# The sum of squares of four RMSNorms moved into the steps that produce the residual, in a hybrid decoder layer

## The chip, the cores and the metric

The kernel runs on all 8 cores of one Trainium2 chip. Two cores share one sequence of 8192 tokens; each has 4096 tokens, and 128 tokens ahead of them (the halo), whose keys, values and conv state it needs. There is no exchange between cores. The metric is the device time of the slowest core, in microseconds (us).

## The reference

One layer over `x` of (4, 8192, 1024), float32, then a final RMSNorm:

```
h = x + 1/2 * SwiGLU_1(RMSNorm(x))                      # d_ff 2816
u = RMSNorm(h);  q,k,v,B,C,xc = u @ W_in
attn = sliding_window_attention(rope(q), rope(k), v)    # window 128, blocks of 128
conv = B * causal_depthwise_conv3(C * xc)
h = h + concat(RMSNorm(attn), RMSNorm(conv)) @ W_out
h = h + CrossAttn(RMSNorm(h), RMSNorm(mem))             # 256 memory tokens
h = h + 1/2 * SwiGLU_2(RMSNorm(h))
out = RMSNorm(h)
# RMSNorm(x) = x * rsqrt(mean(x*x) + 1e-5) * gain, over the 1024 features
```

## The kernel before

**Layout.** A core works in 4 passes of 1024 tokens. The residual `h` stays in SBUF as float32 with features on partitions: 8 chunks of 128 features by 1024 tokens. A pass is cut into two sub-tiles of 512 tokens (`SUB`), s = 0 and 1. Weights stream through a ring in SBUF, by POOL's DMA queue; a load waits until TensorE is done with what stood there. `x` and the output go by SP's queue in blocks of 128 tokens, each through two staging buffers. In pass 0 the halo's 128 tokens are a third, small sub-tile (`hh`, `uh`, `acth`) in FFN1 and in the mixer's input.

**A pass.** `ffn` (norm, input product, SiLU gate, output product), `mixer` (norm, input product with rotary and conv, attention, output product), `xattn` (norm, query product, attention, output product), `ffn` again, `final_out`. The input product of an FFN is 11 weight tiles with 64 matmuls each (4 groups of 8 for the gate and 8 for the product), the longest dense stretch of a pass.

**A norm.** `rmsnorm_to_u` runs for every sub-tile ahead of the stage that uses it. It calls `rms_stats_fm`: for each of the 8 feature chunks, ScalarE squares the chunk into one of two bf16 buffers (`tmpb`), and TensorE multiplies it by a matrix of ones, which adds over the partitions and leaves the sum in all of them, accumulated over the chunks in one PSUM bank. Then Ln and Exp on ScalarE give the reciprocal root (`lnv`, `rstd`), and 8 `scalar_tensor_tensor` on VectorE write `u = h * gain * rstd`. Squares of one sub-tile and scalings of the other may run side by side. The helpers record the operation, so in the profile every matmul is L366, every activation L384, a transpose L370, a copy L406 (ScalarE) or L407 (VectorE).

**The residual loops.** The output products of FFN1, mixer, cross-attention and FFN2 run over m (8 output chunks) and then over s: a group of 22 (FFN) or 8 matmuls of 512 columns into one PSUM bank, and VectorE adds it to `h` (`h` L401 in the FFNs, `h` L388 in the other two). Banks 0 to 5 rotate; 6 and 7 belong to the attention's output.

**The block loops.** `load_x` (pass 0) and `final_out` (between passes) take 8 blocks of 128 tokens. `x_tr` transposes a block of `x` in two halves of four 128x128 pieces, and copies half 0 by VectorE and half 1 by ScalarE into `h`. `final_out` first transposes `h` back for the output (`identf,h`), squares it on ScalarE with a row sum, adds the two sums (`small`), takes Ln and Exp, multiplies by the gain (`stage<-ps,small,gfin`) and sends the block out; then it calls `x_tr` for the next pass's block.

**What sets the order.** Each engine runs its instructions in the order in which the program records them, and waits by semaphores for what the recorder found an operation to need. There is no scheduler: where a matmul stands in the code is where it stands in TensorE's queue.

```
def rms_stats_fm(src_chunks, n, nfeat):
    ...
    for i, s in enumerate(src_chunks):
        sq = nxt("tmpb", tmpb)[:, 0:n]
        act_fn(sq, s, AF.Square)
        mm(ssp, ones, sq, i == 0, i == nchunk - 1)
```

Of the kernel before, what the change touches and what calls it, by code (L numbers as in the profile page):

```python
# [9 lines left out]
AF = mybir.ActivationFunctionType  # L10
# [210 lines left out]
def build_program(cfg):  # L221
# [63 lines left out]
    a = [scr_addr]  # L285
# [221 lines left out]
    def x_dma(row0):  # L507
        stg = nxt("xstage", xstage)
        ldma(stg[:, :], x_d.ap()[row0:row0 + 128, :])
        return stg  # L510

    def x_tr(stg, hdst, bi):
        for half in range(2):
            b = bank()
            for q in range(4):
                kc = half * 4 + q
                tr(ps[:, b, q * 128:(q + 1) * 128], stg[:, kc * 128:(kc + 1) * 128], identf[:, :])
            v_copy(hdst[:, half * 4:half * 4 + 4, bi * 128:(bi + 1) * 128],
                   ps[:, b, :].rearrange("p (a c) -> p a c", a=4), eng=("act" if half else "dve"))

    def load_x(row0, nblocks, hdst):
        for bi in range(nblocks):
            x_tr(x_dma(row0 + bi * 128), hdst, bi)

    def ffn(subs, gcol, wi_d, wo_d, hook=None):
        for (hs, us, as_, n) in subs:
            rmsnorm_to_u(hs, us, n, gcol)
        hooks = list(hook()) if hook is not None else []
        for ti in range(FC // 2):
            wt = wtile(KC * 512)  # L530
            wv = wt[:, :].rearrange("p (k n) -> p k n", k=KC)
            wdma(wv[:, :, 0:256], wsrc(wi_d, 0, KC, ti * 256, 256))
            wdma(wv[:, :, 256:512], wsrc(wi_d, 0, KC, DFF + ti * 256, 256))
            for cc in range(2):
                c = ti * 2 + cc
                for (hs, us, as_, n) in subs:
                    bg, bu = bank(), bank()
                    for kc in range(KC):
                        mm(ps[:, bg, 0:n], wv[:, kc, cc * 128:(cc + 1) * 128], us[:, kc, :], kc == 0, kc == KC - 1)
                    for kc in range(KC):  # L540
                        mm(ps[:, bu, 0:n], wv[:, kc, 256 + cc * 128:256 + (cc + 1) * 128], us[:, kc, :], kc == 0, kc == KC - 1)
                    sg = nxt("sgb", sgb)[:, 0:n]
                    act_fn(sg, ps[:, bg, 0:n], AF.Silu)
                    v_tt(as_[:, c, :], sg, ps[:, bu, 0:n], ALU.mult)
            if ti >= 1 and hooks:
                hooks.pop(0)()
        while hooks:
            hooks.pop(0)()
        for tj in range(4):
            wt = wtile(FC * 256)  # L550
            wv = wt[:, :].rearrange("p (k n) -> p k n", k=FC)
            wdma(wv[:, 0:11, :], wsrc(wo_d, 0, 11, tj * 256, 256))
            wdma(wv[:, 11:22, :], wsrc(wo_d, 11 * 128, 11, tj * 256, 256))
            for mmi in range(2):
                m = tj * 2 + mmi
                for (hs, us, as_, n) in subs:
                    b = bank()
                    for kc in range(FC):
                        mm(ps[:, b, 0:n], wv[:, kc, mmi * 128:(mmi + 1) * 128], as_[:, kc, :], kc == 0, kc == FC - 1)
                    v_stt(hs[:, m, :], ps[:, b, 0:n], 0.5, hs[:, m, :], ALU.mult, ALU.add)  # L560

    def rope_tables(col0, ncols, pos_col0):
        thunks = []
# [51 lines left out]
    def mixer(p_idx, main_subs, halo):  # L615
        if halo:
            rmsnorm_to_u(hh, uh, HALO, GC_MIX)
        for (c0, n) in main_subs:
            rmsnorm_to_u(h[:, :, c0:c0 + n], u[:, :, c0:c0 + n], n, GC_MIX)
        toks = []  # L620
        if halo:
            toks.append((uh, HALO, 0, True, None))
# [176 lines left out]
        for tj in range(4):  # L799
            wt = wtile(KC * 256)  # L800
            wv = wt[:, :].rearrange("p (k n) -> p k n", k=KC)
            for g in range(2):
                src = wmo_d.ap()[g * 256:(g + 1) * 256, tj * 256:(tj + 1) * 256].rearrange("(j d) n -> d j n", d=64)
                wdma(wv[g * 64:(g + 1) * 64, 0:4, :], src)
            wdma(wv[:, 4:8, :], wsrc(wmo_d, 512, 4, tj * 256, 256))
            for mmi in range(2):
                m = tj * 2 + mmi
                for (c0, n) in main_subs:
                    b = bank()
                    for kc in range(KC):  # L810
                        mm(ps[:, b, 0:n], wv[:, kc, mmi * 128:(mmi + 1) * 128], bufA[:, kc, c0:c0 + n], kc == 0, kc == KC - 1)
                    v_tt(h[:, m, c0:c0 + n], ps[:, b, 0:n], h[:, m, c0:c0 + n], ALU.add)

    def xattn(main_subs):
        for (c0, n) in main_subs:
            rmsnorm_to_u(h[:, :, c0:c0 + n], u[:, :, c0:c0 + n], n, GC_XATT)
        for tj in range(4):
            wt = wtile(KC * 256)
            wv = wt[:, :].rearrange("p (k n) -> p k n", k=KC)
# [97 lines left out]
    out_ops = []

    def final_out(p_idx, next_load):
        nrow0 = HALO + (p_idx + 1) * T  # L920
        pre = [x_dma(nrow0 + i * 128) for i in range(min(2, NBLK))] if next_load else []
        for bi in range(NBLK):
            stg = nxt("stage", stage)
            bks = [bank(), bank()]
            sm = nxt("small", small)
            for half in range(2):
                for q in range(4):
                    kc = half * 4 + q
                    tr(ps[:, bks[half], q * 128:(q + 1) * 128], h[:, kc, bi * 128:(bi + 1) * 128], identf[:, :])
                act_fn(stg[:, half * 512:(half + 1) * 512], ps[:, bks[half], :], AF.Square, accum=sm[:, half:half + 1])  # L930
            v_tt(sm[:, 2:3], sm[:, 0:1], sm[:, 1:2], ALU.add)
            act_fn(sm[:, 3:4], sm[:, 2:3], AF.Ln, scale=1.0 / D, bias=epsc[:, :])
            act_fn(sm[:, 2:3], sm[:, 3:4], AF.Exp, scale=-0.5)
            for half in range(2):
                v_stt(stg[:, half * 512:(half + 1) * 512], ps[:, bks[half], :], sm[:, 2:3],
                      gfin[:, half * 512:(half + 1) * 512], ALU.mult, ALU.mult)
            r0 = p_idx * T + bi * 128
            o = P.dma("sp", out_d.ap()[r0:r0 + 128, :], stg[:, :], reads=[stg[:, :]])
            out_ops.append(o)
            if next_load:  # L940
# [159 lines left out]
```

How the kernel before makes its waits and increments, by code:

```python
    def emit(self, eng, h, final_wait=()):  # L194
        seen = {}
        for o in self.ops[eng]:
            need = {}
            for d in o.deps:
                assert d.val is not None
                k = d.sem
                if seen.get(k.num, 0) >= d.val:
                    continue
                if need.get(k.num, (None, 0))[1] < d.val:
                    need[k.num] = (k, d.val)
            for num, (k, v) in need.items():
                h.wait_ge(k, v)
                seen[num] = v
            if o.is_dma:
                out, in_ = o.fn
                h.dma_start(out=out, in_=in_).then_inc(o.sem, 16)
            else:
                ins = o.fn(h)
                if o.signals:
                    ins.then_inc(o.sem, 1)
        for d in final_wait:
            if seen.get(d.sem.num, 0) < d.val:
                h.wait_ge(d.sem, d.val)
                seen[d.sem.num] = d.val
```

## Time and profile before

| | us |
|---|---|
| median of 6 runs | 3741.78 |
| lowest, highest run | 3737.97, 3843.55 |
| the profiled execution's own time | 3741.16 |
| its span on the slowest core (core 1) | 3739.6 |
| TensorE busy, VectorE, ScalarE, POOL | 3234.0, 1411.8, 1008.8, 341.0 |
| spans of the 8 cores | 3732.4 to 3739.6 |
| mean granted TensorE clock of core 1 | 0.869 |

The spans of all cores lie within 0.2%. A granted clock of 1.00 is 2.4 GHz and 0.50 is 1.2 GHz; the engine was always at one of the two. "Busy" TensorE in a row includes the end of each matmul, which overlaps the next one's start, so a busy share says less than the spacing of the starts.

### The profile page before, as it was taken

Reading aid. Unit: us, or ns where it says so; the run is one execution under the profiler, and the core shown is the slowest. Engines: PE = TensorE matmul, PEld = TensorE weight load, DVE = VectorE, ACT = ScalarE, POOL = GpSimd, SP = SyncE. Lnnn points to the kernel's source line nnn. Section 1 sums busy time; section 2 is a strip of 40 time slices with the busy share of each in tenths; the row PEclk is TensorE's granted clock in tenths of the full one; section 3 lists DMA queues with packets and bytes.
Section 4 is the critical chain, followed back from the end, with each engine's and each line's share of the span. In section 5 each row is a group of like instructions: output and inputs, shape, how many; then the busy total and the mean of one; then the engine's idle time right before and its main releaser. Section 6 shows DMA issues by size and latency. Waiting matters only on the chain.

```text
span 3739.6 us, 47167 instructions; the slowest of 8 cores (3732.4 to 3739.6 us)
## 1 busy us (share of the span) xinstructions
PE 3234.0 (86%) x15098; PEld 1449.3 (39%) x15098; DVE 1411.8 (38%) x3210; ACT 1008.8 (27%) x2442; POOL 341.0 (9%) x391
## 2 busy tenths in 40 slices
PE   4999868899899877889979977879997997688997
PEld 2454323344444332334444433323443443233444
DVE  1431654421243355441134145453114415544212
ACT  2220253421131125341031024442103102534211
POOL 1011100011101110001101110000110111000110
PEclk7999957799999985879989997679998998577998
DMA  9456312256746540426656643124664665022453
GB/s 159 53 76 74 37 15 25 33 60 74 127 69 86 66 51 1 46 23 79 73 116 94 77 48 35 18 29 50 79 74 111 79 75 54 11 27 31 62 72 76
DMA packets 405726, 228.52 MB, mean 61 GB/s; under 512 B 56944, under 2 KB 396528, under 8 KB 405488
## 3 DMA queue, kind: packets, MB, share of 16 engines
q0 software_dynamic: 393392, 186.67, 43.3%
q1 hardware_dynamic: 12096, 38.83, 3.1%
q8 instruction: 130, 2.13, 0.2%
q14 instruction: 108, 0.88, 0.1%
HBM read 395.35 MB, written 16.78 MB: 110 GB/s over the span
## 4 chain that ended last, share of the span: by engine, by line
PE 73%; ACT 9%; DVE 9%; issue 6%; DMA 2%; DVEq 0%; ACTq 0%; SPq 0%; POOLq 0%
PE ps L366 72%; ACT tmpb L384 3%; DVE u L401 2%; ACT pf L384 2%; ACT pT L406 1%; PE ps L370 1%; DVE bufA L401 1%; DVE small L845 1%; DMA out<-stage 1%; ACT lnv L384 1%; DVE small L717 1%; DMA xstage<-x 1%; DVE pb L394 1%; ACT rstd L384 1%; DVE small L414 1%
## 5 line engine op out<-in xcount | busy, mean ns | idle before, releaser
L366 PE MATMUL ps<-u,wt 128*128 128x512 bf16 x7744 | 1732.6, 385 | 16.3 <-DVE u L401 16.1
L366 PEld LDWEIGHTS ps<-u,wt 128*128 128x128 bf16 x7744 | 764.5, 99 | 956.7 <-issue 88.1
L366 PE MATMUL ps<-act,wt 128*128 128x512 bf16 x2816 | 610.2, 379 | 0.0
L388 DVE TENSOR_TENSOR act<-sgb,ps 128x512 bf16<-128x512 f32 x352 | 240.4, 687 | 809.8 <-PE ps L366 786.5
L384 ACT ACTIVATE sgb<-ps 128x512 f32<-128x512 f32 (+1 forms) x374 | 213.6, 578 | 804.9 <-PE ps L366 792.2
L366 PEld LDWEIGHTS ps<-act,wt 128*128 128x128 bf16 x2816 | 275.2, 98 | 330.4
L366 PE MATMUL ps<-tmpb,cbf 128*128 128x512 bf16 (+1 forms) x473 | 175.0, 428 | 179.8 <-ACT tmpb L384 138.9
L210 POOL DMA_DIRECT2D wt<-w_ffn_in x176 | 154.3, 879 | 1562.0 <-PE ps L366 1557.9
L401 DVE SCALAR_TENSOR_TENSOR h<-ps,h 128x512 f32<-128x512 f32 x128 | 88.6, 692 | 522.1 <-PE ps L366 522.1
L384 ACT ACTIVATE tmpb<-h 128x512 bf16<-128x512 f32 x256 | 148.6, 623 | 467.2 <-PE ps L366 369.8
L401 DVE SCALAR_TENSOR_TENSOR u<-h,gains,rstd 128x512 bf16<-128x512 f32 x256 | 172.5, 746 | 128.9 <-ACT rstd L384 128.9
L384 ACT ACTIVATE pf<-ps,small 128x257 f32<-128x257 f32 (+1 forms) x384 | 184.4, 481 | 47.3 <-DVE small L414 28.4
L366 PE MATMUL ps<-cbf,pb 128*128 128x128 bf16 x768 | 141.4, 288 | 55.6 <-DVE pb L394 47.2
L366 PEld LDWEIGHTS ps<-tmpb,cbf 128*128 128x128 bf16 x473 | 45.7, 107 | 331.9 <-issue 327.3
L406 ACT CAST pT<-ps 128x256 bf16<-128x256 f32 x384 | 142.2, 373 | 103.3 <-PE ps L366 92.8
L394 DVE TENSOR_SCALAR pb<-pf,small 128x256 bf16<-128x256 f32 x384 | 135.5, 353 | 30.4 <-DVE small L414 2.8
L388 DVE TENSOR_TENSOR h<-ps,h 128x512 f32<-128x512 f32 x128 | 88.6, 692 | 141.9 <-PE ps L366 141.9
L384 ACT ACTIVATE stage<-ps 128x512 f32<-128x512 f32 x64 | 38.3, 599 | 339.1 <-PE ps L370 312.4
L717 DVE TENSOR_REDUCE small<-ps 128x1 f32<-128x257 f32 x256 | 106.9, 420 | 49.8 <-PE ps L366 49.4
L210 POOL DMA_DIRECT2D wt<-w_ffn_out x64 | 67.9, 1061 | 579.7 <-PE ps L366 579.7
L366 PE MATMUL ps<-bufA,wt 128*128 128x512 bf16 x512 | 118.0, 395 | 0.0
L366 PEld LDWEIGHTS ps<-cbf,pb 128*128 128x128 bf16 x768 | 63.6, 119 | 120.9 <-issue 107.2
(126 smaller groups left out, 2091.2 us busy)
## 6 DMA issues: line engine op xcount, KB each, us to landing
wt<-w_ffn_in POOLq DMA_DIRECT2D x176, 512.0 KB, 8.6
wt<-w_ffn_out POOLq DMA_DIRECT2D x64, 704.0 KB, 9.3
xstage<-x SPq DMA_DIRECT2D x33, 512.0 KB, 6.0
out<-stage SPq DMA_DIRECT2D x32, 512.0 KB, 2.9
wt<-w_mix_in POOLq DMA_DIRECT2D x48, 256.0 KB, 7.5
wt<-w_xq POOLq DMA_DIRECT2D x16, 512.0 KB, 7.3
wt<-w_xo POOLq DMA_DIRECT2D x16, 512.0 KB, 7.5
wt<-w_mix_in POOLq DMA_DIRECT2D x12, 512.0 KB, 8.6
```

The source lines that it names most:

```text
L210: h.dma_start(out=out, in_=in_).then_inc(o.sem, 16)
L366: return P.op("pe", lambda e: e.matmul(out, lhsT=lhsT, rhs=rhs, start=start, stop=stop), reads=[lhsT, rhs], writes=[out])
L370: return P.op("pe", lambda e: e.transpose(out, in_, ident), reads=[in_, ident], writes=[out])
L384: return P.op("act", lambda e: e.activation(out=out, in_=in_, func=func, scale=scale, **kw), reads=reads, writes=writes)
L388: return P.op("dve", lambda e: e.tensor_tensor(out=out, in0=in0, in1=in1, op=op), reads=[in0, in1], writes=[out])
L394: return P.op("dve", lambda e: e.tensor_scalar(out=out, in0=in0, scalar1=s1, scalar2=None, op0=op0), reads=reads, writes=[out])
L401: return P.op("dve", lambda e: e.scalar_tensor_tensor(out=out, in0=in0, scalar=scalar, in1=in1, op0=op0, op1=op1), reads=reads, writes=[out])
L406: return P.op("act", lambda e: e.copy(out=out, in_=in_), reads=[in_], writes=[out])
L414: return P.op("dve", lambda e: e.reciprocal(out=out, in_=in_), reads=[in_], writes=[out])
L717: P.op("dve", lambda e: e.tensor_reduce(out=sm[:, 0:1], in_=ps[:, b, 0:257], axis=AX.X, op=ALU.max, negate=True), reads=[ps[:, b, 0:257]], ...
L845: P.op("dve", lambda e: e.tensor_reduce(out=sm[:, 0:1], in_=ps[:, b, 0:MEM], axis=AX.X, op=ALU.max, negate=True), reads=[ps[:, b, 0:MEM]], ...
```

## The change

`stats_add` squares one chunk and issues its ones-matmul; `stats_finish` is Ln and Exp on the finished sum. The sums now stand in PSUM bank 6 + s. The residual loops of FFN1, mixer and cross-attention call `stats_add` after each add; `x_tr` squares and sums each half of a block as it is loaded. `rmsnorm_to_u` then only finishes. The halo sub-tile and the final norm keep the old way. The number of squared elements is the same; for the loaded `x` the ones-matmuls are 64 of 128 columns per pass where they were 16 of 512.

```diff
+    def stats_add(s, m, chunk_ap, n):
+        sq = nxt("tmpb", tmpb)[:, 0:n]
+        act_fn(sq, chunk_ap, AF.Square)
+        mm(ps[:, 6 + s, 0:n], ones, sq, m == 0, m == KC - 1)
+
+    def stats_finish(s, n, nfeat):
...
+        act_fn(lv, ps[:, 6 + s, 0:n], AF.Ln, scale=1.0 / nfeat, bias=epsc[:, :])
+        act_fn(rs, lv, AF.Exp, scale=-0.5)
+        return rs
...
-    def rmsnorm_to_u(hsrc, udst, n, gcol):
-        rs = rms_stats_fm([hsrc[:, kc, :] for kc in range(KC)], n, D)
+    def rmsnorm_to_u(hsrc, udst, n, gcol, fused_s=None):
+        if fused_s is None:
+            rs = rms_stats_fm([hsrc[:, kc, :] for kc in range(KC)], n, D)
+        else:
+            rs = stats_finish(fused_s, n, D)
...
-            v_copy(hdst[:, half * 4:half * 4 + 4, bi * 128:(bi + 1) * 128],
-                   ps[:, b, :].rearrange("p (a c) -> p a c", a=4), eng=("act" if half else "dve"))
+            dst = hdst[:, half * 4:half * 4 + 4, bi * 128:(bi + 1) * 128]
+            v_copy(dst, ps[:, b, :].rearrange("p (a c) -> p a c", a=4), eng=("act" if half else "dve"))
+            if fuse:
+                s = (bi * 128) // SUB
+                cc0 = (bi * 128) % SUB
+                sq = nxt("tmpb", tmpb)[:, 0:512].rearrange("p (a c) -> p a c", a=4)
+                act_fn(sq, dst, AF.Square)
+                for q in range(4):
+                    kc = half * 4 + q
+                    mm(ps[:, 6 + s, cc0:cc0 + 128], ones, sq[:, q, :], kc == 0, kc == KC - 1)
...
                     v_stt(hs[:, m, :], ps[:, b, 0:n], 0.5, hs[:, m, :], ALU.mult, ALU.add)
+                    if fuse_next and fs is not None:
+                        stats_add(fs, m, hs[:, m, :], n)
...
                     v_tt(h[:, m, c0:c0 + n], ps[:, b, 0:n], h[:, m, c0:c0 + n], ALU.add)
+                    stats_add(c0 // SUB, m, h[:, m, c0:c0 + n], n)
...
-                x_tr(pre[bi], h, bi)
+                x_tr(pre[bi], h, bi, fuse=True)
```

TensorE's order at the end of FFN1 in pass 1, before (`act,wt` are the output product's matmuls, `tmpb,cbf` the ones-matmuls):

```order
L366 MATMUL ps<-act,wt_182 128x512 x88
L366 MATMUL ps<-act,wt_183 128x512 x88
L366 MATMUL ps<-act,wt_184 128x512 x88
L366 MATMUL ps<-act,wt_185 128x512 x88
L366 MATMUL ps<-tmpb_83,cbf 128x512
L366 MATMUL ps<-tmpb_82,cbf 128x512
```

and with the change:

```order
L366 MATMUL ps<-act,wt_182 128x512 x22
L366 MATMUL ps<-tmpb_83,cbf 128x512
L366 MATMUL ps<-act,wt_182 128x512 x22
L366 MATMUL ps<-tmpb_82,cbf 128x512
L366 MATMUL ps<-act,wt_182 128x512 x22
L366 MATMUL ps<-tmpb_83,cbf 128x512
```

A ones-matmul now stands behind every 22 matmuls, where 16 stood together behind all 352. The mixer's and the cross-attention's loops read alike with groups of 8.

TensorE's order in `final_out` between two passes, before:

```order
L370 MATMUL ps<-identf,h 128x128 x8
L370 MATMUL ps<-identf,xstage_67 128x128 x8
L370 MATMUL ps<-identf,h 128x128 x8
L370 MATMUL ps<-identf,xstage_66 128x128 x8
L370 MATMUL ps<-identf,h 128x128 x8
```

and with the change:

```order
L370 MATMUL ps<-identf,h 128x128 x8
L370 MATMUL ps<-identf,xstage_67 128x128 x4
L366 MATMUL ps<-tmpb_83,cbf 128x128 x4
L370 MATMUL ps<-identf,xstage_67 128x128 x4
L366 MATMUL ps<-tmpb_82,cbf 128x128 x4
L370 MATMUL ps<-identf,h 128x128 x8
```

Between the two halves of an `x` block, and between it and the next block of `h`, four ones-matmuls stand now.

## Rows read from the trace of the kernel before

**Rows 1.** The page, busy us of each engine, share of the span, instructions.
```profile
PE 3234.0 (86%) x15098; PEld 1449.3 (39%) x15098; DVE 1411.8 (38%) x3210; ACT 1008.8 (27%) x2442; POOL 341.0 (9%) x391
```

**Rows 2.** Timeline, mixer out to queries: start, us, engine, line, operation, count [idle <-releaser].
```profile
1528.93 0.59 PE L366 MATMUL ps<-tmpb,cbf 128*128 128x512 bf16 x2
...
1529.20 0.69 DVE L388 TENSOR_TENSOR h<-ps,h 128x512 f32<-128x512 f32 x1 [1.03 <-PE ps L366]
...
1533.67 0.69 ACT L384 ACTIVATE lnv<-ps,epsc 128x512 f32<-128x512 f32 x1 [0.62 <-PE ps L366]
...
1535.18 5.39 DVE L401 SCALAR_TENSOR_TENSOR u<-h,gains,rstd 128x512 bf16<-128x512 f32 x8 [5.29 <-ACT rstd L384]
...
1542.84 5.39 DVE L401 SCALAR_TENSOR_TENSOR u<-h,gains,rstd 128x512 bf16<-128x512 f32 x8 [2.26 <-ACT rstd L384]
...
1548.37 24.55 PE L366 MATMUL ps<-u,wt 128*128 128x512 bf16 x113 [0.28 <-DVE u L401]
```

**Rows 3.** Timeline, pass 1, FFN1's output product to the mixer's input.
```profile
1276.73 0.59 PE L366 MATMUL ps<-tmpb,cbf 128*128 128x512 bf16 x2
...
1281.48 1.28 ACT L384 ACT_TABLE_LOAD   x1 [0.62 <-PE ps L366]
...
1297.48 0.38 PE L366 MATMUL ps<-u,wt 128*128 128x512 bf16 x1 [0.29 <-DVE u L401]
...
1299.05 3.20 PE L366 MATMUL ps<-u,wt 128*128 128x512 bf16 x8
```

**Rows 4.** Timeline, pass 1, the hand-offs between engines around the mixer's output product.
```profile
1498.43 0.60 ACT L384 ACTIVATE tmpb<-ps 128x512 bf16<-128x512 f32 x1 [1.27 <-PE ps L366]
...
1499.18 0.59 PE L366 MATMUL ps<-tmpb,cbf 128*128 128x128 bf16 x4 [0.84 <-ACT tmpb L384]
...
1503.28 0.69 DVE L388 TENSOR_TENSOR h<-ps,h 128x512 f32<-128x512 f32 x1 [1.42 <-PE ps L366]
...
1504.07 0.63 ACT L384 ACTIVATE tmpb<-h 128x512 bf16<-128x512 f32 x1 [3.44 <-DVE h L388]
```

**Rows 5.** Timeline, pass 1, TensorE at a matmul of the rotary embedding.
```profile
1303.13 0.38 PE L366 MATMUL ps<-tmpb,cbf 128*128 128x512 bf16 x1 [0.88 <-ACT tmpb L406]
```

**Rows 6.** Timeline, block loop between passes 1 and 2, to FFN1's input product.
```profile
1897.98 1.04 PE L370 MATMUL ps<-identf,h 128*128 128x128 f32 x8
...
1912.65 1.91 PE L370 MATMUL ps<-identf,h 128*128 128x128 f32 x8
...
1915.51 0.16 DVE L388 TENSOR_TENSOR small<-small 128x1 f32<-128x1 f32 x1 [2.02 <-ACT stage L384]
...
1916.46 1.41 DVE L401 SCALAR_TENSOR_TENSOR stage<-ps,small,gfin 128x512 f32<-128x512 f32 x2 [0.79 <-ACT small L384]
...
1917.79 0.68 DVE L407 COPY h<-ps 128x512 f32<-128x512 f32 x1
...
1954.01 8.36 PE L366 MATMUL ps<-u,wt 128*128 128x512 bf16 x38 [0.29 <-DVE u L401]
```

**Rows 7.** Timeline, pass 0: first load of `x` to FFN1's input product.
```profile
60.20 3.69 PE L370 MATMUL ps<-identf,xstage 128*128 128x128 f32 x16 [8.20 <-DMA xstage<-x]
...
61.39 0.69 DVE L407 COPY h<-ps 128x512 f32<-128x512 f32 x1 [9.03 <-PE ps L370]
...
83.56 0.59 ACT L406 COPY h<-ps 128x512 f32<-128x512 f32 x1 [2.38 <-PE ps L370]
...
88.46 2.19 DVE L401 SCALAR_TENSOR_TENSOR uh<-hh,gains,rstd 128x128 bf16<-128x128 f32 x8 [5.05 <-ACT rstd L384]
...
109.28 2.10 PE L366 MATMUL ps<-u,wt 128*128 128x512 bf16 x9 [0.29 <-DVE u L401]
```

**Rows 8.** Windows (rotary, attention): us; PE, PEld, DVE, ACT, POOL busy; clock; DMA.
```profile
1303.13:1318.40 15.27, 10.88 (x46) 4.37 (x46) 10.26 (x16) 2.94 (x5) 2.64 (x3) 1.00 0.57 52
1388.00:1498.00 110.00, 77.77 (x371) 30.39 (x371) 59.02 (x222) 62.81 (x213) 0.00 (x0) 0.50 0.00 1
```

More of the change, by code:

```diff
@@ L461, in rms_stats_fm @@
         return rs
-    def rmsnorm_to_u(hsrc, udst, n, gcol):
-        rs = rms_stats_fm([hsrc[:, kc, :] for kc in range(KC)], n, D)
+    assert NSUB <= 2
+    def stats_add(s, m, chunk_ap, n):
[3 more added lines that the diff above has]
+    def stats_finish(s, n, nfeat):
+        i_ = rr.get("rstd", 0)
+        rr["rstd"] = i_ + 1
+        lv = lnv[i_ % 2][:, 0:n]
+        rs = rstd[i_ % 2][:, 0:n]
+        act_fn(lv, ps[:, 6 + s, 0:n], AF.Ln, scale=1.0 / nfeat, bias=epsc[:, :])
[6 more added lines that the diff above has]
+            rs = stats_finish(fused_s, n, D)
         for kc in range(KC):
@@ L510, in x_dma, with x_tr @@
         return stg
-    def x_tr(stg, hdst, bi):
+    def x_tr(stg, hdst, bi, fuse=False):
         for half in range(2):
@@ L517, in x_tr, with load_x, ffn @@
                 tr(ps[:, b, q * 128:(q + 1) * 128], stg[:, kc * 128:(kc + 1) * 128], identf[:, :])
-            v_copy(hdst[:, half * 4:half * 4 + 4, bi * 128:(bi + 1) * 128],
-                   ps[:, b, :].rearrange("p (a c) -> p a c", a=4), eng=("act" if half else "dve"))
-    def load_x(row0, nblocks, hdst):
+            dst = hdst[:, half * 4:half * 4 + 4, bi * 128:(bi + 1) * 128]
[8 more added lines that the diff above has]
+                    mm(ps[:, 6 + s, cc0:cc0 + 128], ones, sq[:, q, :], kc == 0, kc == KC - 1)
+    def load_x(row0, nblocks, hdst, fuse=False):
         for bi in range(nblocks):
[L523 to L527, printed above, removed]
+            x_tr(x_dma(row0 + bi * 128), hdst, bi, fuse=fuse)
+    def ffn(subs, gcol, wi_d, wo_d, hook=None, fuse_next=False):
+        for (hs, us, as_, n, fs) in subs:
+            rmsnorm_to_u(hs, us, n, gcol, fused_s=fs)
         hooks = list(hook()) if hook is not None else []
@@ L535, in ffn @@
                 c = ti * 2 + cc
-                for (hs, us, as_, n) in subs:
+                for (hs, us, as_, n, fs) in subs:
                     bg, bu = bank(), bank()
@@ L555, in ffn @@
                 m = tj * 2 + mmi
-                for (hs, us, as_, n) in subs:
+                for (hs, us, as_, n, fs) in subs:
                     b = bank()
@@ L618, in mixer @@
         for (c0, n) in main_subs:
-            rmsnorm_to_u(h[:, :, c0:c0 + n], u[:, :, c0:c0 + n], n, GC_MIX)
+            rmsnorm_to_u(h[:, :, c0:c0 + n], u[:, :, c0:c0 + n], n, GC_MIX, fused_s=c0 // SUB)
         toks = []
@@ L812, in mixer @@
                     v_tt(h[:, m, c0:c0 + n], ps[:, b, 0:n], h[:, m, c0:c0 + n], ALU.add)
+                    stats_add(c0 // SUB, m, h[:, m, c0:c0 + n], n)
     def xattn(main_subs):
         for (c0, n) in main_subs:
-            rmsnorm_to_u(h[:, :, c0:c0 + n], u[:, :, c0:c0 + n], n, GC_XATT)
+            rmsnorm_to_u(h[:, :, c0:c0 + n], u[:, :, c0:c0 + n], n, GC_XATT, fused_s=c0 // SUB)
         for tj in range(4):
@@ L915, in xattn @@
                     v_tt(h[:, m, c0:c0 + n], ps[:, b, 0:n], h[:, m, c0:c0 + n], ALU.add)
+                    stats_add(c0 // SUB, m, h[:, m, c0:c0 + n], n)
     out_ops = []
@@ L950, in build_program @@
             load_x(0, 1, hh)
-            load_x(HALO, NBLK, h)
+            load_x(HALO, NBLK, h, fuse=True)
             hook = lambda: rope_tables(0, TP, 0)
@@ L959, in build_program @@
         if halo:
-            subs.append((hh, uh, acth, HALO))
+            subs.append((hh, uh, acth, HALO, None))
         for (c0, n) in main_subs:
-            subs.append((h[:, :, c0:c0 + n], u[:, :, c0:c0 + n], act[:, :, c0:c0 + n], n))
-        ffn(subs, GC_FFN1, w1i_d, w1o_d, hook=hook)
+            subs.append((h[:, :, c0:c0 + n], u[:, :, c0:c0 + n], act[:, :, c0:c0 + n], n, c0 // SUB))
+        ffn(subs, GC_FFN1, w1i_d, w1o_d, hook=hook, fuse_next=True)
         mixer(p_idx, main_subs, halo)
         xattn(main_subs)
-        subs2 = [(h[:, :, c0:c0 + n], u[:, :, c0:c0 + n], act[:, :, c0:c0 + n], n) for (c0, n) in main_subs]
+        subs2 = [(h[:, :, c0:c0 + n], u[:, :, c0:c0 + n], act[:, :, c0:c0 + n], n, c0 // SUB) for (c0, n) in main_subs]
         ffn(subs2, GC_FFN2, w2i_d, w2o_d)
```

## The prediction

> **What bounds the kernel now.** I read the page first: TensorE is busy 86% of a span of 3739.6 us, the other engines below 40% [rows 1]. So what counts is what holds TensorE up. Next I read the timeline around one norm, the mixer's exit into the cross-attention (pass 1), since the change touches norms. TensorE's last output matmul ends at about 1528.93 us, where the norm's own ones-matmuls begin; the scaling of `u` for sub-tile 0 starts at 1535.18, for sub-tile 1 at 1542.84, and the last matmul that waits for such a `u` starts at 1548.37: the norm holds the dense stream up for 19.44 us [rows 2]. The same norm after FFN1 takes 20.75 us, with a table load of 1.28 us ahead of its Ln [rows 3]. The one ahead of FFN2 looks like the first. Last I read what a dependent matmul costs an in-order TensorE [rows 4, 5], and the two loops that load `x` [rows 6, 7].
>
> A difference of under 0.2% (7.5 us) can't be told from no change here. The sum is made against the profiled execution's own 3741.16 us, which lies 0.6 us under the median of the six runs shown.
>
> **Residual loops (FFN1 out, mixer out, cross-attention out).** For each output chunk m and sub-tile s, the stream was 22 or 8 matmuls, then the next group's. Now one ones-matmul stands between them, and it needs this group's own result: last matmul, the add on VectorE, Square on ScalarE, ones-matmul. TensorE has nothing else in its queue, since the next group's matmuls stand behind. The wait, from rows:
> - last matmul's start to the start of the add: 0.49 us. The ones-matmul at 1528.93 started as the last output matmul had streamed its 0.217 us (113 matmuls in 24.55 us), and the add started at 1529.20 [rows 2];
> - the add 0.69 us; 0.10 to the Square; Square 0.63 [rows 4];
> - Square's end to the ones-matmul: 0.15 (1498.43 + 0.60 to 1499.18) [rows 4];
> - the ones-matmul itself: 0.22.
>
> That is 2.28 us from the last matmul of a group to the first of the next, where it was 0.22: **2.06 us more per group**, 1.84 of it idle. There are 16 groups per loop, 3 loops, 4 passes. The last group's wait I count with the norm behind it, so 15 x 3 x 4 = 180 groups: **+371 us**. That presumes TensorE at 2.4 GHz. The add and the Square cost nothing more: ScalarE was idle in these loops and VectorE did the add before. No DMA is moved, and POOL's weight loads, which wait for TensorE to free the ring, merely come later with it. PSUM banks 6 and 7, which hold the sums now, are used by attention alone and free by then.
>
> **The norms behind these loops.** The 16 Squares and ones-matmuls go; Ln, Exp and the 16 scalings stay. From the end of the last output matmul (t = 0), cross-attention case: add 0.27 to 0.96, Square 1.06 to 1.69, ones-matmul at 1.84. Ln of sub-tile 0 needs none of this and stands behind the last Square in ScalarE's queue, so it starts at 1.69. From Ln's start to the scaling is 1.51 us (1533.67 to 1535.18), so `u` of sub-tile 0 starts at 3.20, and Ln and Exp of sub-tile 1 hide beside it. Now VectorE is the bound: 8 scalings in 5.39 us, then 8 more, the last awaited matmul 5.53 us after their start (1542.84 to 1548.37) [rows 2]: 3.20 + 5.39 + 5.53 = 14.1 us instead of 19.44. After FFN1 the table load comes first: 15.4 instead of 20.75 [rows 3]. So a norm gives back only 5.3 us, not the 10 us of Squares taken out, because the Squares of sub-tile 1 already ran beside the scaling of sub-tile 0. 12 norms: **-64 us**.
>
> **The block loop between passes** (`final_out` with the next load, 8 blocks, 3 times). Before, the transposes of `x` run ahead of ScalarE and VectorE; with the norm behind it, the stretch from the first transpose to the last awaited matmul is 1897.98 to 1954.01, 56.0 us [rows 6]. Now each half's ones-matmuls wait for that half's copy and Square. With the clock at 1.2 GHz, which TensorE's little work here makes likely, one block from its first transpose: 2.86 us to the add of the two halves' sums (1912.65 to 1915.51), 0.95 to the gain multiply (to 1916.46), 1.33 to the copy of half 0 (to 1917.79) [rows 6]; copy 0.68, hand-off 0.10, Square 0.63, hand-off 0.15, four ones-matmuls about 0.43; four transposes to the copy about 1.2 (as 60.20 to 61.39 [rows 7]), copy 0.59, 0.10, Square 0.63, 0.15, 0.43. Sum 10.2 us; at 2.4 GHz the same comes to 8.8. Eight blocks to the last Square (the first still at the higher clock, with one table load) are 80.6 us, and the norm behind it now 1.6 + 5.39 + 5.53 = 12.5: 93 against 56, **+37 us** each, +111 in all; at the higher clock +28 each. The output DMAs have more time, not less.
>
> **The first load.** Its second block is in at 60.2 us, its last copy starts at 83.56 [rows 7]. A fused block takes about 3.2 + 3.1 = 6.3 us by the pieces above, so the seven from there end at 104 instead of 84. From there the halo norm's 4.4 us (to 88.46) and its scaling 2.2 stay, then 5.4 + 5.5: 121 against 109.28, **+12 us** (0 if the early loads hide it, 20 if they add to it).
>
> **The clock.** A fused norm feeds TensorE one matmul per 0.66 us for 11 us. Before, such a stretch of some 4 us ended at 1.2 GHz after FFN1: the next 8 matmuls took 3.20 us instead of 1.73 [rows 3]. Where the clock had come back before the dense stream (the other 12 norms, those ahead of FFN1 included), I charge one such stretch, 1.7 us: **+20 us** (0 to 40).
>
> Sum: 371 - 64 + 111 + 12 + 20 = +450, so **4190 us**. The case's own ends: down to 4117 with the boundary at 2.4 GHz (-27), no clock charge (-20), the load free (-12) and 1.98 us per group (-14); up to 4250 with both clock charges double (+20, and +16 for a slow second group at the start of the mixer's and the cross-attention's loops), 2.12 us per group (+11) and the load at 20 (+8).
>
> **Rivals.**
> 1. *The clock falls in the short loops.* In mixer out and cross-attention out TensorE would stream 1.95 of 3.79 us. For it: the attention loop with TensorE "busy" 77.77 of 110 us had a granted clock of 0.50 [rows 8]. Against: the rotary stretch, idle 0.88 us in each 3 us, had 1.00 [rows 5, 8]; my loop lies between. At 1.2 GHz a group takes 7 x 0.43 + 0.70 + 0.69 + 0.10 + 0.63 + 0.15 + 0.43 = 5.7 us, 1.9 more; 120 groups: +230, 4420 us. The Trainium skill ("TensorE: Matmul & The Clock Gate", A second HAM failure mode) has a rule that speaks for this rival: small idles between groups of matmuls, taken often enough, make the gate swing between its two levels. By it the short loops would lose all or part of those 230 us; the trace agrees for attention and not for the rotary stretch. Chance 6%.
> 2. *The block loops hide the waits.* If they were set by ScalarE's work alone, two more Squares of 0.63 per block would cost 10 us and the shorter norm give back 8: 4075 us. Against it, each piece of the chain waits for the one before. Chance 3%.
> 3. *The waits are covered, and the kernel gets faster.* If TensorE ran the next group's matmuls while the ones-matmul waits, the residual loops would keep their time, the norms give back 64, the block loops and the first load 32, less 20 for the clock: about 3665 us. It decides in the residual loops together with the block loop: with only the former covered the rest still adds 79; with both, the break-even lies at 0.4 us per group. Against: in the rotary stretch the next group's matmuls stand ready behind a matmul that waits for ScalarE, and TensorE idles 0.88 us all the same [rows 5]. Chance 3%, of which 1 within 0.2%.
>
> **Numbers.** The forecast has 88%. The range 4120 to 4260 holds its own ends nearly; left out are the three rivals (12%) and its own tail. Faster 2%, within 0.2% 1%, slower 97%.
>
> **What would show it.** In the waits, TensorE for ScalarE's `tmpb` should stand at over 400 us in total; the residual loops should show groups 3.8 us (8 matmuls) and 6.8 us (22) apart with granted clock 1.00; rows like those of 1542.84 should start 5.4 us after the first scaling; a block between passes 9 to 10 us. Groups 1.8 us apart, or 5.7, would make me wrong, and so would a block under 6 us.

## The result, and the profile after

| | before | with the change |
|---|---|---|
| median of the runs, us | 3739.74 (6 runs, 3737.97 to 3743.49) | 4193.56 (5 runs, 4189.34 to 4194.18) |
| ratio, with its 95% interval | | 1.121 [1.1195, 1.1226] |
| span of the core that is read, us | 3739.6 | 4186.4 |

The change makes the kernel 12% slower. The forecast was 4190 us. Some runs of every kernel show a lower granted clock and longer spans on one die or both; times and means over cores leave those runs and dies out, and the rows of after are of core 0 because cores 4 to 7 were like that in its execution. An experiment below that has no ratio rests on one or two runs.

The page's head and busy line, and the group of the ones-matmuls (last two numbers: idle time ahead of them in all, and what of it ScalarE's `tmpb` ended):

```profile
span 4186.4 us, 47522 instructions; the slowest of 8 cores (4185.2 to 4382.4 us)
...
PE 3301.0 (79%) x15290; PEld 1476.3 (35%) x15290; DVE 1411.0 (34%) x3210; ACT 1019.8 (24%) x2442; POOL 340.3 (8%) x391
...
L366 PE MATMUL ps<-tmpb,cbf 128*128 128x128 bf16 (+1 forms) x665 | 161.9, 333 | 594.9 <-ACT tmpb L384 559.2
```

Against [rows 1] no engine has much more to do: VectorE is where it was, ScalarE has 11 us more, and TensorE has 192 matmuls more (the 128-column ones of the block loops) and 67 us more busy time. The span grew by 447 us, so 380 of them are idle time of TensorE. The waits say for what (engine, what it waits for, us in total, times, longest):

```profile
PE ps L366 <- ACT tmpb L384: 559.2, 311, 6.0
ACT tmpb L384 <- DVE h L388: 417.2, 128, 5.1
ACT tmpb L384 <- DVE h L401: 413.5, 64, 7.9
```

The first row was 138.9 us in 170 waits before (its longest 3.5 us). The three rows are one ring: TensorE waits for the Square, the Square for the add, and the add, in rows not shown, for TensorE.

**Residual loops.** TensorE in FFN1's output product (start, us, operation, count, idle and its releaser):

```profile
1366.65 0.38 PE L366 MATMUL ps<-tmpb,cbf 128*128 128x512 bf16 x1 [1.78 <-ACT tmpb L384]
1366.86 4.91 PE L366 MATMUL ps<-act,wt 128*128 128x512 bf16 x22
1373.55 0.38 PE L366 MATMUL ps<-tmpb,cbf 128*128 128x512 bf16 x1 [1.78 <-ACT tmpb L384]
1373.76 4.91 PE L366 MATMUL ps<-act,wt 128*128 128x512 bf16 x22
1380.45 0.38 PE L366 MATMUL ps<-tmpb,cbf 128*128 128x512 bf16 x1 [1.78 <-ACT tmpb L384]
```

Every 22 matmuls are followed by 1.78 us in which TensorE is idle; groups stand 6.90 us apart. The hand-offs of one group of the mixer's output product, in time order over three engines:

```profile
1675.25 0.69 DVE L388 TENSOR_TENSOR h<-ps,h 128x512 f32<-128x512 f32 x1 [3.19 <-PE ps L366]
1676.15 0.63 ACT L384 ACTIVATE tmpb<-h 128x512 bf16<-128x512 f32 x1 [3.25 <-DVE h L388]
...
1676.92 0.38 PE L366 MATMUL ps<-tmpb,cbf 128*128 128x512 bf16 x1 [1.77 <-ACT tmpb L384]
...
1677.13 1.89 PE L366 MATMUL ps<-bufA,wt 128*128 128x512 bf16 x8
```

The add ends at 1675.94 and the Square starts at 1676.15, 0.21 us later, where [rows 4] have 0.10. Windows of FFN1 out, mixer out, cross-attention out, and six blocks of the block loop (us; busy and count of PE, PEld, DVE, ACT, POOL; granted clock; DMA share; GB/s):

```profile
1332.30:1440.93 108.63, 81.57 (x367) 35.30 (x366) 11.07 (x16) 9.44 (x15) 10.50 (x11) 1.00 0.48 55
1672.00:1720.00 48.00, 25.64 (x110) 10.47 (x111) 8.37 (x13) 8.18 (x13) 2.62 (x3) 1.00 0.28 33
1821.00:1875.00 54.00, 29.23 (x126) 11.65 (x125) 9.69 (x14) 8.81 (x14) 3.49 (x4) 1.00 0.34 39
1103.09:1163.57 60.48, 27.48 (x146) 23.02 (x145) 13.00 (x24) 22.31 (x54) 0.00 (x0) 0.50 0.29 102
```

The granted clock is 1.00, that is 2.4 GHz, in these windows of all three residual loops, with TensorE busy for 25.64 of 48.00 us in the second; in the block loop it is 0.50, that is 1.2 GHz. The windows of the mixer and the cross-attention leave out the first group of the loop, which still runs slowly behind the attention:

```profile
1660.50 3.23 PE L366 MATMUL ps<-bufA,wt 128*128 128x512 bf16 x8
```

Eight matmuls take 3.23 us there instead of 1.89. The kernel before has the same slow start (granted clock 0.94 over its whole loop), so it costs the change nothing.

**The norm behind the mixer**, which answers to [rows 2]:

```profile
1719.92 1.89 PE L366 MATMUL ps<-bufA,wt 128*128 128x512 bf16 x8
...
1721.92 0.69 DVE L388 TENSOR_TENSOR h<-ps,h 128x512 f32<-128x512 f32 x1 [3.19 <-PE ps L366]
...
1722.82 0.63 ACT L384 ACTIVATE tmpb<-h 128x512 bf16<-128x512 f32 x1 [3.25 <-DVE h L388]
...
1723.35 0.67 ACT L384 ACTIVATE lnv<-ps,epsc 128x512 f32<-128x512 f32 x1
...
1723.59 0.38 PE L366 MATMUL ps<-tmpb,cbf 128*128 128x512 bf16 x1 [1.78 <-ACT tmpb L384]
...
1724.85 10.69 DVE L401 SCALAR_TENSOR_TENSOR u<-h,gains,rstd 128x512 bf16<-128x512 f32 x16 [2.23 <-ACT rstd L384]
```

The last output matmul has streamed by 1721.66 (1719.92 and eight times 0.217). All 16 scalings run without a gap from 1724.85 to 1735.54, so from the end of that matmul to the last `u` it is 13.9 us, with the hand-off to TensorE about 14.0, where it was 19.44. VectorE is now the bound of the norm. What it does to the clock, in windows from the first matmul on the new `u`:

```profile
1725.74:1735.60 9.86, 8.77 (x15) 1.54 (x15) 9.86 (x16) 0.30 (x1) 0.00 (x0) 0.50 0.17 20
1735.60:1741.00 5.40, 5.32 (x20) 2.22 (x20) 1.23 (x2) 0.71 (x2) 0.47 (x1) 0.75 0.00 0
1741.00:1760.00 19.00, 19.00 (x90) 8.59 (x88) 4.15 (x6) 2.94 (x6) 3.03 (x4) 1.00 0.70 77
```

While each matmul waits for a scaling the clock stands at 0.50, which costs nothing: a scaling comes every 0.67 us and a matmul takes 0.43. In the 5.40 us behind, 20 matmuls run where 5.40 / 0.217 = 25 would: 1.1 us lost.

**The block loop**, which answers to [rows 6]: one block, and the last norm behind the loop.

```profile
1163.57 1.91 PE L370 MATMUL ps<-identf,h 128*128 128x128 f32 x8
...
1166.43 0.16 DVE L388 TENSOR_TENSOR small<-small 128x1 f32<-128x1 f32 x1 [7.08 <-ACT stage L384]
...
1167.37 1.41 DVE L401 SCALAR_TENSOR_TENSOR stage<-ps,small,gfin 128x512 f32<-128x512 f32 x2 [0.79 <-ACT small L384]
...
1168.70 0.68 DVE L407 COPY h<-ps 128x512 f32<-128x512 f32 x1
...
1169.47 0.63 ACT L384 ACTIVATE tmpb<-h 128x512 bf16<-128x512 f32 x1 [2.20 <-DVE h L407]
...
1170.25 0.58 PE L366 MATMUL ps<-tmpb,cbf 128*128 128x128 bf16 x4 [3.91 <-ACT tmpb L384]
...
1174.48 10.69 DVE L401 SCALAR_TENSOR_TENSOR u<-h,gains,rstd 128x512 bf16<-128x512 f32 x16 [4.80 <-ACT rstd L384]
...
1185.32 4.91 PE L366 MATMUL ps<-u,wt 128*128 128x512 bf16 x22 [0.29 <-DVE u L401]
```

The transposes of `h` start at 1103.09 and, six blocks on, at 1163.57: 10.1 us a block. From the first transpose of the loop (1092.23) to the last matmul that waits for a scaling (1185.32) it is 93.1 us, where it was 56.0 [rows 6]. Every step stands behind the one before it, 5.13 us to the copy of half 0 (1163.57 to 1168.70) and 1.55 from there to its ones-matmuls.

### The profile page after: what moved, and what is told of

The parts are those of the page before. It is cut to its first block, busy times and chain, and to the rows that moved or that the text cites. A ratio compares the mean times of both kernels' runs of the same rounds, so it can differ in the third digit from the quotient of the medians.

```text
span 4382.4 us, 47522 instructions; the slowest of 8 cores (4185.2 to 4382.4 us)
## 1 busy us (share of the span) xinstructions
PE 3500.0 (80%) x15290; PEld 1523.8 (35%) x15290; DVE 1411.0 (32%) x3210; ACT 1019.7 (23%) x2442; POOL 341.8 (8%) x391
## 3 DMA queue, kind: packets, MB, share of 16 engines
q8 instruction: 131, 2.15, 0.2%
## 4 chain that ended last, share of the span: by engine, by line
PE 71%; DVE 11%; ACT 10%; issue 7%; DMA 1%; ACTq 0%; DVEq 0%; SPq 0%; POOLq 0%
PE ps L366 69%; ACT tmpb L384 4%; DVE h L388 2%; PE ps L370 2%; ACT pf L384 2%; DVE h L401 1%; ACT pT L406 1%; DVE small L875 1%; DVE bufA L401 1%; DVE u L401 1%; DVE small L746 1%; DVE pb L394 1%; DVE small L414 1%; ACT lnv L384 1%; ACT stage L384 1%
## 5 line engine op out<-in xcount | busy, mean ns | idle before, releaser
L366 PE MATMUL ps<-u,wt 128*128 128x512 bf16 x7744 | 1899.6, 406 | 46.8 <-DVE u L401 35.4
L366 PEld LDWEIGHTS ps<-u,wt 128*128 128x128 bf16 x7744 | 789.3, 102 | 1107.1 <-issue 507.4
L366 PE MATMUL ps<-act,wt 128*128 128x512 bf16 x2816 | 666.6, 400 | 0.0
L366 PE MATMUL ps<-tmpb,cbf 128*128 128x128 bf16 (+1 forms) x665 | 167.7, 342 | 594.1 <-ACT tmpb L384 558.4
L366 PEld LDWEIGHTS ps<-act,wt 128*128 128x128 bf16 x2816 | 285.8, 102 | 357.8 <-issue 125.3
L384 ACT ACTIVATE tmpb<-h 128x512 bf16<-128x512 f32 x256 | 161.1, 629 | 988.9 <-DVE h L388 468.4
L366 PEld LDWEIGHTS ps<-tmpb,cbf 128*128 128x128 bf16 x665 | 60.4, 114 | 778.8 <-issue 777.6
L366 PE MATMUL ps<-bufA,wt 128*128 128x512 bf16 x512 | 164.8, 480 | 0.0
```

The lines of the kernel that those rows point to most:

```text
L366: return P.op("pe", lambda e: e.matmul(out, lhsT=lhsT, rhs=rhs, start=start, stop=stop), reads=[lhsT, rhs], writes=[out])
L384: return P.op("act", lambda e: e.activation(out=out, in_=in_, func=func, scale=scale, **kw), reads=reads, writes=writes)
```

## The experiments

Nine kernels, each against the kernel before. A ratio has its 95% interval.

**1. The residual loops alone.** The block loops and the first load keep the old way, and FFN1's norm squares for itself. **2. The loads alone**, the complement: `stats_add` out of the three residual loops.

```diff
 # 1
-            rmsnorm_to_u(hs, us, n, gcol, fused_s=fs)
+            rmsnorm_to_u(hs, us, n, gcol, fused_s=(None if fuse_next else fs))
-                x_tr(pre[bi], h, bi, fuse=True)
+                x_tr(pre[bi], h, bi)
-            load_x(HALO, NBLK, h, fuse=True)
+            load_x(HALO, NBLK, h)
 # 2
-                    stats_add(c0 // SUB, m, h[:, m, c0:c0 + n], n)
-                        stats_add(fs, m, hs[:, m, :], n)
```

> Only the residual loops of FFN1, mixer and cross-attention are fused; the loaded x is squared ahead of FFN1 as before. Theory (TensorE waits behind each ones-matmul): 180 groups at 2.06 to 2.13 us, 371 to 385, less 64 for the 12 norms, plus up to 20 for the clock: about 4070 us, 4045 to 4090. If the block loops carried more of the loss than I worked out, this run would come out under 4000.

> Only the block loops (first load and between passes) are fused; residual loops and the other norms as before. Theory: 37 us for each of 3 block loops and 12 for the first load, 3 to 5 for the clock: about 3870 us, 3850 to 3880. Its difference and that of the residual-only run should add up to the whole change's 451 us within 10. If the block loop hides the waits: 3750.

Measured: 4072.78 us and 3859.14 us, one run each, against 3738.79 before on the same chip. The excesses are 334 and 120 us; together 454, and the change as a whole has 454 (4193.56 less 3739.74). The two parts add up, and each lies where its theory had it. In the waits TensorE's wait for `tmpb` is 418.1 us with the residual loops alone and 278.4 us with the loads alone.

**3. The ones-matmul one group later.** Kernel 1, but a group's ones-matmul is issued behind the matmuls of the next group, ahead of that group's add. All Squares, ones-matmuls and sums are the same; only the place in TensorE's queue differs.

```diff
-        mm(ps[:, 6 + s, 0:n], ones, sq, m == 0, m == KC - 1)
+        late.append((ps[:, 6 + s, 0:n], sq, m == 0, m == KC - 1))
+
+    def stats_late():
+        while late:
+            o_, sq_, a_, b_ = late.pop(0)
+            mm(o_, ones, sq_, a_, b_)
...
+                    stats_late()
                     v_tt(h[:, m, c0:c0 + n], ps[:, b, 0:n], h[:, m, c0:c0 + n], ALU.add)
                     stats_add(c0 // SUB, m, h[:, m, c0:c0 + n], n)
```

> As the residual-only run, but each ones-matmul is issued one group later, behind the next group's 22 or 8 matmuls. Theory (the loss is the wait and nothing else): the waits are covered except the last of a loop, so the norms' gain remains: 3742 - 64 + up to 20 = 3680 to 3700 us. Rival (the loss is the interruption itself: the ones-matrix loaded into the array among the weights, the extra PSUM bank or the clock): it stays near the residual-only run, over 4000 us.

Measured: 3725.07 us (3722.40 to 3727.34), ratio 0.9964 [0.995, 0.9977]. The wait is gone, and with it 348 us; but the time misses its range by 25 us on the slow side. TensorE in the mixer's output product:

```profile
1522.92 0.38 PE L366 MATMUL ps<-tmpb,cbf 128*128 128x512 bf16 x1
1523.15 1.89 PE L366 MATMUL ps<-bufA,wt 128*128 128x512 bf16 x8
1524.87 0.38 PE L366 MATMUL ps<-tmpb,cbf 128*128 128x512 bf16 x1
1525.09 1.89 PE L366 MATMUL ps<-bufA,wt 128*128 128x512 bf16 x8
```

and the windows of FFN1's and the mixer's output products:

```profile
2099.30:2178.10 78.80, 78.80 (x366) 35.71 (x365) 11.06 (x16) 9.45 (x15) 10.51 (x11) 1.00 0.59 75
1498.40:1530.50 32.10, 32.10 (x143) 13.74 (x142) 11.50 (x19) 10.07 (x17) 2.62 (x3) 0.95 0.40 50
```

No idle is left, and still FFN1's loop takes 78.80 us where it took 75.76 before, the mixer's 32.10 where it took 29.16 (start of the first output matmul to start of the last). That is 3.0 us a loop, some 14 ones-matmuls of 0.22 us. Before, they stood in the norm, each within TensorE's wait for the next Square, and cost nothing; now they stand in a dense stretch and cost what they take. Over 180 groups: 40 us; the twelve loops together are 41 us longer in the mean of the cores. The norms give back some 58 (below), and 3739 - 58 + 41 = 3722.

**4. No dependence.** Kernel 1 again, the ones-matmul at its early place, but reading a fixed tile of ones. The Squares are still computed. This kernel leaves the true sums out: every norm behind a residual loop divides by a constant.

```diff
+    fixed, _, _ = P.sb("fixed", [128, 512], BF16, alias=masks_addr)
...
-        mm(ps[:, 6 + s, 0:n], ones, sq, m == 0, m == KC - 1)
+        mm(ps[:, 6 + s, 0:n], ones, fixed[:, 0:n], m == 0, m == KC - 1)
```

> As the residual-only run, each ones-matmul at its fused place, but it reads a fixed tile of ones instead of the squared chunk, so it waits for nothing (Squares are still computed; the norm's sums are a constant). Theory: same instructions, no wait, so within 25 us of the run with the late ones-matmul, 3660 to 3700 us. Rival (interruption, not wait): over 4000 us.

Measured: 3722.19 us (3721.20 to 3726.59), ratio 0.9959 [0.9942, 0.9977]. It lies above the range, as kernel 3 does and for the same cause: its FFN1 loops are longer by 13 us over the four passes and its mixer loops by 13, as in kernel 3 by 15 and 12. The two kernels are within 3 us of each other. So of the 387 us by which the residual loops grew, the ones-matmuls themselves are 40, and the other 347 are the wait of a matmul at the head of TensorE's queue. The order of the matmuls, the extra PSUM banks and ScalarE's work in the loops are not among the causes, since this kernel has them all. Moving the ones-matmul by one group removes all of the wait.

**5. The block loops late as well.** Kernel 3, with the fused load; a block's Squares come behind the next block's output work, and its ones-matmuls behind the next block's transposes.

```diff
+            if next_load and bi > 0:
+                blk_squares(bi - 1)
...
-                x_tr(pre[bi], h, bi, fuse=True)
+                x_tr(pre[bi], h, bi)
+                stats_late()
```

> Residual loops as in the run with the late ones-matmul, and the block loops too: a block's Squares come behind the next block's Exp, its ones-matmuls behind the next block's transposes. Theory (the block loops lose by the wait as well): the whole change's 118 us there vanish, and the norm ahead of FFN1 gives back up to 8 us at each of 3 boundaries, less what two more Squares per block cost ScalarE: 3700 to 3730 us. Rival (ScalarE or the DMAs bound the block loop once Squares stand in it): over 3750 us.

Measured: 3709.98 and 3711.54 us, against 3741.78 to 3745.93 before on that chip. TensorE in the middle of the block loop between passes 1 and 2:

```profile
1906.88 0.90 PE L366 MATMUL ps<-tmpb,cbf 128*128 128x128 bf16 x8 [1.85 <-ACT tmpb L384]
1907.62 1.04 PE L370 MATMUL ps<-identf,h 128*128 128x128 f32 x8
...
1911.46 0.90 PE L366 MATMUL ps<-tmpb,cbf 128*128 128x128 bf16 x8 [1.67 <-ACT tmpb L384]
1912.20 1.04 PE L370 MATMUL ps<-identf,h 128*128 128x128 f32 x8
```

A block takes 4.58 us here instead of 10.1, with all the same instructions; others of this loop take up to 7.1, and from the first transpose (1886.60) to the last awaited matmul (1940.90) it is 54.3 us, where the kernel before had 56.0 and the changed one 93.1. The shorter waits are not all of the 5.5 us a block: eight transposes take 1.04 us here and 1.91 in the changed kernel, so the clock has come back too (0.96 granted from 1902.60 to 1916.77). The prediction's estimate of a fused block at the higher clock is 8.8 us, so the clock may account for 1.4 of the 5.5; no run separates the two. The time lies in its range. The fused load, which cost 120 us in kernel 2, now gives back some 14 (3725 to 3711), 5 of them in the first load.

**6. The first weight tile by sub-tile.** Kernel 5, where in the first weight tile behind a norm both chunks of sub-tile 0 go ahead of sub-tile 1, so that TensorE has work while VectorE scales sub-tile 1.

```diff
-            for cc in range(2):
+            grp = [(cc, sb_) for cc in range(2) for sb_ in subs]
+            if ti == 0:
+                grp = [(cc, sb_) for sb_ in subs for cc in range(2)]
+            for (cc, sb_) in grp:
```

> As the run with everything late, and in the first weight tile of each input product sub-tile 0 does both its chunks before sub-tile 1 begins. Theory (behind a norm the 16 scalings on VectorE, 10.7 us, are the bound, and TensorE waits for sub-tile 1's): 8 more matmuls, 1.7 us, cover that wait at each of 16 norms, so 20 to 28 us less than the run before it, 3675 to 3705 us. If VectorE is not the bound there: no difference.

Measured: 3692.45 and 3692.60 us, ratio 0.9859 [0.9817, 0.9902]; 18 us less than kernel 5 (14 in the mean span of the cores), under the 20 to 28 expected. The gain isn't spread over the 16 norms as the theory had it. The cross-attention's query product, behind the mixer's norm, is 2.8 us shorter in each pass, 11 of the 14 us; the input products behind the other three norms change by about 0.5 us or less a pass. So the scalings of sub-tile 1 can be covered in this way at one of the four norms; why not at the others stays open.

**7. The sum over chunks on VectorE.** Kernel 1 with kernel 6's order of the first weight tile, but VectorE adds the squared chunks and TensorE does one ones-matmul per sub-tile instead of eight.

```diff
+        acc = lnv[s][:, 0:n]
+        if m == 0:
+            act_fn(acc, chunk_ap, AF.Square)
+            return
...
+            s, dst, sq, acc, m, n = late.pop(0)
+            v_tt(dst, sq, acc, ALU.add)
+            if m == KC - 1:
+                mm(ps[:, 6 + s, 0:n], ones, dst, True, True)
```

> Residual loops only, with the new order of the first weight tile. VectorE adds up the squared chunks as they come (7 adds of 128x512 per sub-tile, each one group late), and one ones-matmul per sub-tile closes a norm instead of 8. Theory (a ones-matmul in a dense stretch costs its own 0.22 us, which it did not in the norm, where TensorE waited for ScalarE): against the run with the late ones-matmul 14 x 12 x 0.22 = 36 us less, 7 more for the longer tail, 20 to 28 less by the order: 3665 to 3685 us. Rival (VectorE, at 1.4 of 1.73 us in the short loops, becomes the bound): over 3710 us.

Measured: 3668.11 us (3665.26 to 3668.22), ratio 0.9792 [0.9763, 0.982]. The mixer's output loop, and the norm behind it:

```profile
1481.20:1509.90 28.70, 28.59 (x125) 12.65 (x126) 18.65 (x31) 9.74 (x17) 2.63 (x3) 0.95 0.44 56
```

```profile
1511.80 0.38 PE L367 MATMUL ps<-accb,cbf 128*128 128x512 bf16 x1 [1.54 <-DVE accb L389]
...
1513.84 10.69 DVE L402 SCALAR_TENSOR_TENSOR u<-h,gains,rstd 128x512 bf16<-128x512 f32 x16 [1.14 <-ACT rstd L385]
...
1515.40 8.99 PE L367 MATMUL ps<-u,wt 128*128 128x512 bf16 x21 [0.27 <-DVE u L402]
```

The loop takes 28.70 us, no more than before the change: the ones-matmuls have left the dense stretch, and VectorE has the room, busy 18.65 of 28.70 us. Over the four passes FFN1's loops take 311.6 us and the mixer's 116.5, where they took 311.6 and 116.4 before the change and 327.1 and 128.7 in kernel 3. So the 41 us that kernel 3 had lost are back, and with the 14 of the order 3725 - 41 - 14 = 3670. The two edits were made together in this kernel; it is the times of the stages that tell them apart.

**8. Kernel 7 with kernel 5's block loops.**

```diff
-                x_tr(pre[bi], h, bi, fuse=True)
+                x_tr(pre[bi], h, bi)
+                blk_late()
+                if bi == NBLK - 1:
+                    blk_squares(bi)
```

> The run with the sum on VectorE, and the block loops with late Squares and ones-matmuls as in the run with everything late. Theory: the gains add, some 14 us less than the former (what everything late gained over residual loops late): 3645 to 3662 us, faster than both kernels of this study. If the block loops' gain was the order's or chance: 3665 us, as the former.

Measured: 3654.13 us (3653.87 to 3656.54), ratio 0.9765 [0.9746, 0.9784]. It beats both kernels, the one before by 88 us and the changed one by 539, and kernel 7 by 14, as expected.

**9. Squares into a buffer of their own.** Kernel 1, where the Squares of FFN1's and the mixer's loops go into chunks of `u` that are dead by then, instead of the two `tmpb`. A Square then waits for its add alone, and no longer for what used its buffer two groups back.

```diff
-        sq = nxt("tmpb", tmpb)[:, 0:n]
+        sq = u[:, m, s * SUB:s * SUB + n] if own else nxt("tmpb", tmpb)[:, 0:n]
```

> The residual-only run, with the Squares of FFN1's and the mixer's loops written into the dead chunks of u instead of the two tmpb buffers (16 chunks, none used twice in a loop). In the trace of the whole change the Square starts 0.21 us after the add where I had counted 0.10. Theory (the Square waits on two semaphores, the add's and the one that frees its buffer, and the second costs 0.11 us): groups of FFN1 at 6.79 and of the mixer at 3.77 us, those of the cross-attention stay at 3.88; 120 groups less 0.11, 10 to 14 us under the residual-only run, about 4058 us. If 0.21 is what this hand-off costs: no difference.

Measured: 4062.86 us (4058.06 to 4066.03), ratio 1.0853 [1.0822, 1.0885]. One group of the mixer's loop:

```profile
1642.81 0.69 DVE L388 TENSOR_TENSOR h<-ps,h 128x512 f32<-128x512 f32 x1 [3.07 <-PE ps L366]
1643.59 0.63 ACT L384 ACTIVATE u<-h 128x512 bf16<-128x512 f32 x1 [3.14 <-DVE h L388]
...
1644.37 0.38 PE L366 MATMUL ps<-u,cbf 128*128 128x512 bf16 x1 [1.67 <-ACT u L384]
...
1648.14 0.38 PE L366 MATMUL ps<-u,cbf 128*128 128x512 bf16 x1 [1.67 <-ACT u L384]
```

The Square starts 0.09 us after the add, and the groups stand 3.77 us apart where they were 3.88. In the changed kernel the first two groups of the mixer's loop, whose `tmpb` no group of the loop has used yet, are 3.77 us apart as well (ones-matmuls at 1665.39 and 1669.16 us). That leaves 13 groups of a loop that can gain; over 2 loops and 4 passes 0.11 us make 11 us. The FFN1 and mixer loops are 9.4 us shorter than in kernel 1 (mean of the cores, all passes), and the time is 10 us shorter, against the one run of kernel 1.

The expectation spoke of two semaphores, a second one costing 0.11 us. The trace shows three. In the changed kernel ScalarE's queue holds three semaphore waits ahead of the Square of 1676.15, at 1675.97, 1676.03 and 1676.08 us: one on VectorE's count (the add), one on ScalarE's own (what it wrote to the buffer before) and one on TensorE's (what read the buffer). The Squares of the first two groups, and all of these loops in this kernel, have the first alone. So it is two more waits of 0.055 us each. In the changed kernel 168 Squares have all three and start 0.20 us after their add in the median; those with one start 0.09 us after.

## Why the prediction was right, step by step

The forecast said 4190 us and the likeliest case came in. Its terms against what the traces show, stage by stage, in the mean of the cores:

| term | predicted, us | measured, us |
|---|---|---|
| residual loops, 180 groups | 2.06 each, +371 | 2.15 each, +387 |
| 12 norms, with the clock behind 8 of them | -64 and 8 x 1.7 | -58 |
| three block loops, with the clock behind | +111 and 5 | +109 |
| first load, with the clock behind | +12 and 2 | +12 |
| sum | +450 | +450; the time of the slowest core +454 |

- **Residual loops.** The chain of five pieces was right, its place too: the wait for `tmpb` is 559.2 us where over 400 was asked for. FFN1's loop went from 75.76 to 108.63 us, the mixer's from 29.16 to 61. One piece was mis-sized: the hand-off from the add to the Square, taken as 0.10 us from [rows 4], measured 0.21, because the Square also has to wait for its buffer, by two more semaphore waits: with a buffer of its own (experiment 9) it starts 0.09 us after the add. The row I had read was of a norm's first Square, which has one semaphore wait only. Groups are 3.88 and 6.90 us apart, not 3.8 and 6.8 (3.77 and 6.79 between the first two of a loop). Experiments 3 and 4 show that of the 387 us the wait is 347 and the ones-matmuls 40, where the sum had 331 and 40 (1.84 and 0.22 us a group).
- **Norms.** The whole norm behind the mixer came as worked out (14.0 us, predicted 14.1), with VectorE's 16 scalings as its bound; the second eight follow without a gap. The clock was charged too high: 1.7 us behind eight norms, where the window behind the mixer's shows 1.1. From the last output matmul to the end of the next input product the stages are 5.2 (FFN1), 3.9 (mixer) and 5.3 us (cross-attention) shorter a pass. So the mixer's norm loses some 1.4 of its 5.3 us and the cross-attention's next to nothing, and the 12 norms give back 58 us rather than 50. In the sum the loops were 16 us too low, the norms 7, the block loops 7 and the first load 2 too high (with their clock); that it is within 4 us of the time is partly luck.
- **Block loops.** A block took 10.03 to 10.3 us behind the first, predicted 10.2, at the granted clock of 0.50 that the estimate presumed, and the stretch 93.1 us, predicted 93. From FFN2's last output matmul to FFN1's first the three boundaries grew by 35.9, 37.5 and 33.6 us (core 0 against core 1 of before).
- **Rival 1, the clock in the short loops**, is out: the windows show 1.00 in all three loops, and the one slow group at the start of the mixer's and the cross-attention's is in the kernel before too. The Trainium skill ("TensorE: Matmul & The Clock Gate", A second HAM failure mode) tells of a kernel in which small idles between groups of matmuls made the gate swing; 1.78 us of idle in every 3.88 did not do it in these loops. Attention's 0.50 [rows 8] is not explained by the presence of idles alone.
- **Rival 2, block loops that hide the waits**, is out by experiment 2: 120 us for the loads alone. With the waits moved by order (experiment 5) the stretch is back to 54.3 us from 93.1. So they were what set the loop, directly and, as far as the clock came back with them, through it.
- **Rival 3, covered waits**, is out for the change, and experiments 3 and 5 show what it would have been worth. Its price was wrong: I had said that the residual loops "would keep their time", and 3665 us. With everything covered the kernel takes 3711, 46 us more. 40 of them are the ones-matmuls themselves, which had cost nothing in the old norm's waits; rival 3 took them to cost nothing in the dense stretch as well. The expectations of experiments 3 and 4 had the same mistake in them and missed by it.

Why the loops' wait exceeds what the norm gave back by so much: the old norm waited for 16 Squares once, two at a time in a pipeline of ScalarE and TensorE, 10 us of it and half of that beside the scalings. The fused one goes through the whole chain add, Square, matmul 16 times, with nothing beside it.

## What to carry to other kernels

In a queue that runs in order, an operation that depends on the group just finished costs the whole round trip over the other engines each time; issue it one group later, behind independent work, and the wait is gone (here 348 us, by moving one matmul in the queue). Moving work out of a wait into a dense stretch is not free: it then costs its own time (here 41 us), and if another engine has room it can go there (VectorE here took it over at no loss in the loops). And what a stage gives back when part of it is taken out is set by its next bound, here 16 scalings of 0.67 us, so count that before counting what is removed.

## What was not expected of the hardware

- A Square that waits for an add and for its buffer started 0.20 to 0.21 us after the add, one that waits for the add alone 0.09 to 0.10 us, though the buffer had been free for over 6 us (its last reader, the ones-matmul of two groups back, started at 1669.16 us for the Square of 1676.15). The difference is two semaphore waits in ScalarE's queue, 0.055 us each, for things that are long past.
- The granted clock held at 1.00 over 48 and 54 us with TensorE busy about half the time (25.64 of 48.00 and 29.23 of 54.00 us) in steady groups, and stood at 0.50 where single matmuls came 0.66 us apart for 10 us. What makes the difference stays open: no experiment varied it.
